# Attention computed by pairs of heads, with gate tiles of the input projection placed among its steps

## The chip, the cores and the metric

The kernel runs on one core of one Trainium2 chip. The metric is the device time of one execution in microseconds (us). Three runs of the kernel before gave 3889.78, 3900.20 and 3900.45 us, median 3900.2 us. The engines are named as in the profile: PE is TensorE, DVE is VectorE, ACT is ScalarE, POOL is GpSimd, SP is SyncE.

## The reference

The reference is a first block (pooling, two convolution branches, a gated feed-forward layer) followed by a second block of two layers. The change lies in the second block. There are 256 latent tokens x and 256 context tokens xc, the model width is 2048. Each layer does, cut to what matters:

```python
u = h @ w_in       # h: normalized x (and xc); columns of u: qa ka va qb kb vb cq ckv kpe z
# a: 8 heads of 64, latent queries see a neighbourhood (bias rpb) plus all context keys
# b: 12 heads of 64 on 4 key heads, window of 128 plus all context keys, one sink logit per head
# c: 6 heads, 192 wide keys (128 + 64 rotary), 128 wide values, from low-rank projections
s = q @ k.T * scale + bias
p = softmax(s)
o = p @ v
y = concat(o_a, o_b, o_c) * silu(z)
x = x + gate * (y @ w_out)
```

Latent queries read 512 keys, context queries read the 256 context keys. In layer 0 both streams are computed (4 blocks of 128 queries), in layer 1 only the latent one (2 blocks), since no later layer reads the context. gate, shift and scale come from c @ w_ada, 24 blocks of 512 columns for both layers.

## The kernel before

All weights come as one stream of quarters of 512 KB (128 x 1024 f32). Each quarter that feeds the projections is split on the fly: ACT copies it to a rounded high part (`hi`, L656), DVE subtracts to get the low part (`lo`, L978), and PE makes three fp32r products for each of 8 chunks (`tile`, L1513 to L1515). A tile of 128 output columns takes two quarters, 48 matmuls, of 512 tokens in layer 0 and of 256 in layer 1 (except keys and values, which always have 512). `hi` and `lo` run AHEAD=3 quarters before PE. Quarters of w_ada are used unsplit by `mod_quarters` (L1540), in four groups of 32 columns; they are woven between tiles by `weave`.

Each layer runs, one after the other: the z tiles (16, `z0`/`z1`; in layer 1 with 32 quarters of w_ada, 8 ahead and 24 among the tiles), the projections of a (12 tiles), attention a, the projections of b (10), attention b, the projections of c (11 tiles and 21 smaller ones), attention c, then the output projection (16 tiles, `out0`/`out1`). A z tile is finished by a sigmoid on ACT (L708) and a product on DVE (L1452).

Attention works by units of one head and 128 queries: a0 has 32 units, b0 48, c0 24, a1 16, b1 24, c1 12. Its steps, in a pipeline several units deep, with two or four PSUM banks for each product:

- PE scores (L1758) into one of four banks; a head of a or b uses 64 of the array's 128 rows, the lower or the upper half
- DVE bias (L1393) or window mask (L1399), maximum (L1401), its negative (L1404; with the sink L1406)
- ACT exponential with row sum (L907; the sink's own, L906)
- DVE reciprocal (L1417) and scaling (L1420)
- PE transposes of the probabilities (L1768), ACT copies them out of PSUM (L916)
- PE values (L1778; 64 of the array's columns for a and b), DVE product with the gate (L1426)

Every engine runs its instructions in program order, and order between engines is set by semaphores: PE's scores of unit n wait for the exponential of unit n-4, its transposes for DVE's scaling, its values for ACT's copy. `projected` and `attention` exist once for each engine and are called in turn:

```python
for name in "abc":
    projected(name, l)
    attention(f"{name}{l}")
```

PE waits between them for the last value transpose (`vt_used`) and for DVE's stage semaphore.

Of the kernel before, what the change touches and what calls it, by code (L numbers as in the profile page):

```python
# [34 lines left out]
S_BANK = (4, 5, 0, 1)  # L35
T_BANK, O_BANK = (6, 2), (7, 3)
BIASES = 4
# [72 lines left out]
Z_MODS = [sum(len(e["pre"]) + len(e["mods"]) for e in w) for w in Z_WEAVE]  # L110
assert FF_GROUPS * FFN_BLOCKS + sum(Z_MODS) // 8 == ADA_BLOCKS

# [12 lines left out]
NQ = _q  # L125

# [7 lines left out]
def _converted():  # L134


    of = []
    for name, nq, _ in PHASES:
        own = set()
        if name == "ffn":  # L140
            own = {FFN_Q * g + pos for g in range(FF_GROUPS) for e in FFN_WEAVE for pos, _ in e["mods"]}
        elif name in ("z0", "z1"):
            l = int(name[1])
            own = {pos for e in Z_WEAVE[l] for pos, _ in e["pre"] + e["mods"]}
        of += [Q0[name] + k for k in range(nq) if k not in own]
    return of
# [64 lines left out]
def build(nc, stream, xT, ctxT, params, consts, natten, out):  # L211
# [68 lines left out]
    probs = sb("probs", [4, 2 * S], F32, "work", 0)  # L280
    probsT = sb("probsT", [3, 4 * P], F32, "work", 8 * KIB)
    bias = sb("bias", [BIASES, S], F32, "q", 16 * KIB)

# [10 lines left out]
    with ExitStack() as ctx:  # L294
# [269 lines left out]
        units, UNITS_OF = [], {}  # L564
        biases = []

        def unit(l, kind, h, qt):
# [3 lines left out]
            u = dict(no=len(units), kind=kind, nk=nk, k0=k0, q0=q0, bias=None, sink=None)  # L571
            if kind == "a":
                a, c = HD * (h % 2), h // 2
                u.update(qk=[(qkv[a:a + HD, c, q0:q0 + P], qkv[a:a + HD, 4 + c, k0:k0 + nk])],
                         v=P * c + a, nv=HD, p0=a, y=c, scale=HD ** -0.5)
                if not ctx_q:
                    u["bias"] = len(biases)
                    biases.append((l, h, qt))
            elif kind == "b":
                c, a = h // 2, HD * (h % 2)  # L580
                t = c // 3
                u.update(qk=[(qkv[a:a + HD, c, q0:q0 + P], qkv[a:a + HD, 6 + t, k0:k0 + nk])],
                         v=P * t + a, nv=HD, p0=a, y=4 + c, scale=HD ** -0.5,
                         sink=H_B * l + B_ORDER[h])
                if not ctx_q:
                    u["swa"] = qt
            else:
                a = HD * (h % 2)
                u.update(qk=[(cqk[:, h, q0:q0 + P], cqk[:, KN + h, k0:k0 + nk]),
                             (cqk[a:a + HD, QROPE + h // 2, q0:q0 + P], cqk[a:a + HD, KR + h // 2, k0:k0 + nk])],  # L590
                         v=P * h, nv=P, p0=0, y=10 + h, scale=QK_C ** -0.5)
            units.append(u)

        for l in range(LAYERS):
            for kind, heads_ in (("a", H_A), ("b", H_B), ("c", H_C)):
                start = len(units)
# [11 lines left out]
        SIG = {"conf": 0, "sconv": 8, "br_c": 16, "br_a": 32, "br_b": 48, "ffn": 64, "z0": 64 + FF_CH, "z1": 80 + FF_CH}  # L608
# [36 lines left out]
        def _(act):  # L645
# [224 lines left out]
            def projected(name, l):  # L870
                tiles_, items = projections(name, l)
                first = T0[f"{name}{l}"]
                for u, todo in enumerate(items):
                    s, nq = tiles_[u][0:2] if u < len(tiles_) else (None, 0)
                    if nq:
                        hi(SQ.index(s) + AHEAD)

                    for it in sorted(todo, key=lambda it: it[0] != "sq"):
                        if it[0] == "fin":
                            root(it[1])  # L880
                        elif it[0] == "vt":
                            n = it[1]
                            act.wait_ge(vt_ready, n + 1)
                            act.activation(vtok[:, :, vts[n][1]:vts[n][1] + P],
                                           psum[:, 7, :].rearrange("p (t c) -> p t c", t=4),
                                           ACT.Copy).then_inc(vt_used, 1)
                        elif it[0] == "cat" and it[2] < len(jobs[it[1]]["cat"]):
                            cat_hi_part(jobs[it[1]], it[2])
                        elif it[0] == "sq":
                            act.wait_ge(psum_free, copied(first, it[4]))  # L890
                            squares(it[1], it[2], it[3])
                    if nq == 2:
                        hi(SQ.index(s) + 1 + AHEAD)

            def attention(name):
                us = UNITS_OF[name]
                for step in range(len(us) + 3):
                    if step < len(us):
                        u = units[us[step]]
# [1178 lines left out]
```

## Time and profile before

| | us |
|---|---|
| median of three runs | 3900.2 |
| the profiled execution | 3891.74 |
| its span | 3889.8 |
| PE busy | 3654.3 (94%) |
| DVE busy | 2197.5 (56%) |
| ACT busy | 1416.3 (36%) |
| mean granted clock of PE | 0.956 |

Busy time of PE is modelled from pipelined matmuls, so it includes short gaps. PEclk 1.00 is 2.4 GHz, 0.50 is 1.2 GHz. "Idle before" is the time in which an engine had nothing to do before an instruction, with what ended it. Stages are named by heads and layer: b0 is attention b of layer 0.

### The profile page before, as it was taken

The page shows a single profiled execution, that of the slowest core. Times are in us where ns is not written, and L with a number is a line of the kernel's source. Part 1 is how long each engine was busy: PE and PEld are TensorE (multiplying, and loading weights), DVE is VectorE, ACT ScalarE, POOL GpSimd, SP SyncE. Part 2 cuts the span into 40 slices and gives each one's busy share as a digit, 9 for nine tenths or more (in the row PEclk, how much of TensorE's full clock was granted, in tenths as well). Part 3 has the DMA queues.
Part 4 walks back from the last instruction along what each step waited for, and adds up shares of the span by engine and source line. Part 5 has one row for each costly group of instructions (what it writes and reads, how often), then busy time and mean ns, then how long its engine had stood idle before and what let it go on. Part 6 is the DMA issues. An engine that isn't in the chain of part 4 may idle for free.

```text
span 3889.8 us, 62805 instructions
## 1 busy us (share of the span) xinstructions
PE 3654.3 (94%) x23040; PEld 3075.4 (79%) x23040; DVE 2197.5 (56%) x3342; ACT 1416.3 (36%) x2126; POOL 583.1 (15%) x558
## 2 busy tenths in 40 slices
PE   7998997999999999999999999998889899999878
PEld 6997996999878788888888676685468687768648
DVE  4566764557646465665426566637643455774744
ACT  4433443445323233344422333423332442443332
POOL 0395995112000000002000000000001000000000
PEclk9998998999999999999999898999899999999979
DMA  4553553555767677767322111021022562212214
GB/s 169 184 182 133 184 182 105 184 194 174 253 213 239 223 245 238 243 230 243 130 98 92 60 65 45 17 76 64 33 88 96 206 232 94 91 39 85 86 43 148
DMA packets 157143, 554.61 MB, mean 143 GB/s; under 512 B 17392, under 2 KB 21488, under 8 KB 156912
## 3 DMA queue, kind: packets, MB, share of 16 engines
q1 hardware_dynamic: 151680, 532.57, 40.7%
q0 software_dynamic: 5232, 18.88, 1.4%
q8 instruction: 155, 2.54, 0.3%
q14 instruction: 76, 0.62, 0.1%
HBM read 545.09 MB, written 6.29 MB: 142 GB/s over the span
## 4 chain that ended last, share of the span: by engine, by line
PE 74%; DVE 8%; POOLq 6%; POOL 5%; ACT 2%; issue 2%; DMA 2%; DVEq 1%; ACTq 0%; SPq 0%
PE psum L1513 19%; PE psum L1514 18%; PE psum L1515 18%; POOLq L1836 6%; PE psum L1758 4%; POOL conv L1837 4%; PE psum L1540 3%; PE psum L1778 3%; DVE rst L1009 2%; PE psum L1768 2%; PE psum L1608 1%; DVE wlo L978 1%; DMA raw<-in_stream 1%; ACT whi L656 1%; PE psum L1550 1%
## 5 line engine op out<-in xcount | busy, mean ns | idle before, releaser
L1513 PE MATMUL psum<-hcat,whi 128*128 128x256 f32 (+1 forms) x5516 | 1743.6, 316 | 66.4 <-DVEq L967 30.9
L1514 PE MATMUL psum<-hcat,whi 128*128 128x256 f32 (+1 forms) x5516 | 1718.8, 312 | 3.2 <-issue 3.2
L1515 PE MATMUL psum<-hcat,wlo 128*128 128x256 f32 (+1 forms) x5516 | 1718.7, 312 | 0.0
L978 DVE TENSOR_TENSOR wlo<-raw,whi 128x1024 fp32r<-128x1024 f32 (+3 forms) x844 | 1034.2, 1230 | 867.2 <-ACT whi L656 840.0
L656 ACT ACTIVATE whi<-raw 128x1024 fp32r<-128x1024 f32 (+3 forms) x844 | 865.5, 1029 | 1280.9 <-PE psum L1515 925.7
L1513 PEld LDWEIGHTS psum<-hcat,whi 128*128 128x128 f32 x5516 | 1067.6, 194 | 197.4 <-issue 107.4
L1514 PEld LDWEIGHTS psum<-hcat,whi 128*128 128x128 f32 x5516 | 1067.7, 194 | 55.8 <-issue 3.8
L1515 PEld LDWEIGHTS psum<-hcat,wlo 128*128 128x128 f32 x5516 | 1066.9, 193 | 56.4 <-issue 3.4
L1835 POOL TENSOR_SCALAR tap<-glu,par 128x255 f32<-128x255 f32 (+9 forms) x180 | 223.0, 1239 | 0.0
L1009 DVE RECIPROCAL rst<-rst 128x512 f32<-128x512 f32 (+1 forms) x65 | 181.1, 2787 | 41.9 <-ACT rst L677 41.9
L1513 PE MATMUL psum<-thirdcat,whi 128*128 128x256 f32 x687 | 201.0, 293 | 0.0
L1514 PE MATMUL psum<-thirdcat,whi 128*128 128x256 f32 x687 | 194.7, 283 | 0.0
L1515 PE MATMUL psum<-thirdcat,wlo 128*128 128x256 f32 x687 | 194.5, 283 | 0.0
L1822 POOL TENSOR_TENSOR thirdcat<-tmp,thirdcat 128x256 fp32r<-128x256 f32 x51 | 54.0, 1059 | 852.5 <-ACT thirdcat L702 852.4
L1837 POOL TENSOR_TENSOR conv<-conv,tap 128x255 f32<-128x255 f32 (+9 forms) x180 | 167.6, 931 | 28.0 <-issue 2.6
L1513 PEld LDWEIGHTS psum<-thirdcat,whi 128*128 128x128 f32 x687 | 131.6, 192 | 50.3 <-issue 41.1
L1778 PE MATMUL psum<-probsT,vtok 128*64 128x128 f32 (+1 forms) x1040 | 159.1, 297 | 11.2 <-ACT probsT L916 10.6
L1906 POOL DMA_DIRECT2D X<-resid_dram x2 | 2.4, 1180 | 1072.7 <-DVEq L967 1072.7
L1540 PE MATMUL psum<-raw,cs 128*32 128x512 f32 x768 | 159.9, 609 | 0.0
L1778 PEld LDWEIGHTS psum<-probsT,vtok 128*64 128x64 f32 (+1 forms) x1040 | 125.1, 160 | 36.2 <-ACT probsT L916 20.6
L907 ACT ACTIVATE probs<-psum,stat 128x512 f32<-128x512 f32 (+1 forms) x156 | 94.8, 607 | 160.0 <-DVE stat L1404 160.0
L1768 PEld LDWEIGHTS psum<-con,probs 128*128 128x128 f32 x520 | 59.3, 151 | 110.2 <-DVE probs L1420 59.9
(179 smaller groups left out, 3250.2 us busy)
## 6 DMA issues: line engine op xcount, KB each, us to landing
raw<-in_stream SPq DMA_DIRECT2D x978, 512.0 KB, 3.9
raw<-in_stream SPq DMA_DIRECT2D x18, 384.0 KB, 3.0
raw<-in_stream SPq DMA_DIRECT2D x24, 256.0 KB, 2.6
X<-in_ctxT POOLq DMA_DIRECT2D x2, 2048.0 KB, 13.4
resid_dram<-X POOLq DMA_DIRECT2D x2, 2048.0 KB, 12.3
bias<-in_natten POOLq DMA_DIRECT2D x32, 128.0 KB, 2.3
X<-resid_dram POOLq DMA_DIRECT2D x2, 2048.0 KB, 9.9
raw<-in_stream SPq DMA_DIRECT2D x16, 192.0 KB, 2.5
```

The source lines that it names most:

```text
L656: act.activation(whi[:, c % HI_SLOTS, 0:n], raw[:, slot, 0:n], ACT.Copy).then_inc(hi_ready, 1)
L978: vec.tensor_tensor(wlo[:, slot, 0:n], raw[:, slot, 0:n], whi[:, c % HI_SLOTS, 0:n].bitcast(F32), ALU.subtract).then_inc(lo_ready, 1)
L1009: vec.reciprocal(r, r)
L1513: pe.matmul(dst, h, cat[:, kk, c0:c0 + width], start=(q == 0 and k == 0), stop=False)
L1514: pe.matmul(dst, h, cat[:, kk, c0 + loff:c0 + loff + width], start=False, stop=False)
L1515: last = pe.matmul(dst, l_, cat[:, kk, c0:c0 + width], start=False, stop=(q == nq - 1 and k == nch - 1))
L1540: last = pe.matmul(psum[32 * g:32 * g + 32, 4 + a // 8 % 2, :], cs[:, j, :], raw[:, s % SLOTS, 512 * k:512 * k + 512], start=(j < 4), stop ...
L1758: last = pe.matmul(psum[:, S_BANK[no % 4], 0:u["nk"]], q, k, start=(m == 0), stop=(m == len(u["qk"]) - 1))
L1778: last = pe.matmul(psum[u["p0"]:u["p0"] + u["nv"], O_BANK[no % 2], 0:P], vtok[:, u["k0"] // P + c, u["v"]:u["v"] + u["nv"]], probsT[:, no ...
L1835: pool.tensor_scalar(tap[:, t % 2, 0:S - t], pick(glu, c, 0, S - t), wt, None, ALU.mult)
L1836: pool.drain()
L1837: pool.tensor_tensor(pick(conv, c, t, S), pick(conv, c, t, S), tap[:, t % 2, 0:S - t], ALU.add)
```

## The change

1. Attention works by pairs of heads. A pair of a or b has one head in each half of the array: its two score products stand next to each other in the program, use rows 0 to 63 and 64 to 127 and write two banks; its value products alternate between columns 0 to 63 and 64 to 127 of one bank. DVE and ACT handle both heads in one instruction where they can (bias, maximum, negative, reciprocal, copy of the transposes, gate product); the exponentials and the scaling stay one for each head.
2. There is one set of banks for pairs (scores 2 and 3, transposes 4 and 5, values 6), for c a second set for scores (0 and 1). The scores of pair p wait for the exponentials of pair p-1 (for c of p-2).
3. Only 2 z tiles (layer 0) or 4 (layer 1) stay ahead of the projections of a. 6 or 5 go beside attention a, 8 or 7 beside attention b. A z tile has four slots of 12 matmuls each, after which PE may do a step of attention: scores of pair p, values of p-2, transposes of p-1. `beside` deals the steps to the slots. ACT and DVE have the same slots in their own programs, with `hi` or `lo` of one quarter at each even slot, the sigmoid of the tile before at slot 0 of a tile, its product at slot 1.
4. The last value transposes and rotations of the projections of a and b are carried into the first slots.
5. The 24 quarters of w_ada among the z tiles of layer 1 go among the tiles of `out0`. All 8 pairs of chunks of the context's normalized input (`hc1`) now fall in the 4 z tiles that are left.

Of the three functions `attend` in the diff the first is ACT's, the second DVE's, the third PE's.

```diff
+Z_SPLIT = [(2, 6, 8), (4, 5, 7)]
-MOD_Z = [0] + [2] * 12 + [0] * 3
-Z_WEAVE = [weave([2] * KD, [0] * KD), weave([2] * KD, MOD_Z, Z_BEFORE)]
+MOD_OUT = [0] + [2] * 12 + [0] * 3
+Z_WEAVE = [weave([2] * Z_SPLIT[0][0], [0] * KD), weave([2] * Z_SPLIT[1][0], [0] * KD, Z_BEFORE)]
+OUT_WEAVE = weave([2] * KD, MOD_OUT)
...
+        def beside(kind, l):
+            n, slots = len(PAIRS_OF[f"{kind}{l}"]), 4 * Z_SPLIT[l]["ab".index(kind) + 1]
+            at = {2 + p * (slots - 3) // (n + 1): p for p in range(n + 2)}
...
+            def attend(p, us):
+                if 1 <= p <= len(us):
+                    transposed(us[p - 1])
+                if p < len(us):
+                    probabilities(us[p])
...
+                for s in range(4 * n):
+                    if s % 2 == 0:
+                        hi(C0[name] + s // 2 + AHEAD)
+                    if s % 4 == 0 and s:
+                        gate(l, z0 + s // 4 - 1)
+                    if s < len(carry):
+                        for_heads(carry[s], T0[f"{kind}{l}"])
+                    if s in at:
+                        attend(at[s], us)
...
+            def attend(p, us):
+                if 1 <= p <= len(us):
+                    norms(us[p - 1])
+                if p >= 3:
+                    gated(us[p - 3])
+                if p < len(us):
+                    maxima(us[p])
...
+                for s in range(4 * n):
+                    if s % 2 == 0:
+                        lo(C0[name] + s // 2 + AHEAD)
+                    if s % 4 == 1 and s > 1:
+                        z_done(l, z0 + s // 4 - 1)
...
+            def scores(no):
+                u = pairs[no]
+                if no:
+                    pe.wait_ge(exp_ready, no if u["kind"] != "c" else max(no - 1, 1))
+                for m, both in enumerate(u["qk"]):
+                    for h, (q, k) in enumerate(both):
+                        last = pe.matmul(psum[:, s_bank(no) + h, 0:u["nk"]], q, k, start=(m == 0),
+                                         stop=(m == len(u["qk"]) - 1))
...
+            def attend(p, us):
+                if p < len(us):
+                    scores(us[p])
+                if p >= 2:
+                    values(us[p - 2])
+                if 1 <= p <= len(us):
+                    transposes(us[p - 1])
```

On ACT, in attention a of layer 1 before, exponentials (L907) and copies (L916) of single units alternate:

```order
L907 ACTIVATE probs,stat<-psum,stat 128x512 x4
L916 ACTIVATE probsT<-psum 128x512
L907 ACTIVATE probs,stat<-psum,stat 128x512
L916 ACTIVATE probsT<-psum 128x512
L907 ACTIVATE probs,stat<-psum,stat 128x512
```

At the same place now (L701 is `hi`, L753 the sigmoid of a z tile, L957 the exponential, L966 the copy):

```order
L957 ACTIVATE probs,stat<-psum,stat 128x512 x2
L701 ACTIVATE whi<-raw 128x1024
L753 ACT_TABLE_LOAD
L753 ACTIVATE tmp<-psum 128x256
L966 ACTIVATE probsT<-psum 128x1024
L957 ACT_TABLE_LOAD
L957 ACTIVATE probs,stat<-psum,stat 128x512 x2
L701 ACTIVATE whi<-raw 128x1024
L966 ACTIVATE probsT<-psum 128x1024
L957 ACTIVATE probs,stat<-psum,stat 128x512 x2
```

The split of a weight quarter and, for each z tile, a sigmoid with two table loads have moved between the exponentials.

On DVE, in the same stage before, one unit follows the other:

```order
L1417 RECIPROCAL stat<-stat 128x1
L1420 TENSOR_SCALAR probs<-probs,stat 128x512
L1426 TENSOR_TENSOR X<-psum,X 64x128
L1393 SCALAR_TENSOR_TENSOR psum<-bias,psum 128x256
L1401 TENSOR_REDUCE stat<-psum 128x1
L1404 TENSOR_SCALAR stat<-stat 128x1
```

And now (L1053 is `lo`, L1524 the product of a z tile, L1497 and L1501 `norms`, L1510 `gated`, L1471 to L1483 `maxima`):

```order
L1480 TENSOR_REDUCE stat<-psum 128x2
L1483 TENSOR_SCALAR stat<-stat 128x2
L1053 TENSOR_TENSOR wlo<-raw,whi 128x1024
L1524 TENSOR_TENSOR X<-psum,tmp 128x256
L1497 RECIPROCAL stat<-stat 128x2
L1501 TENSOR_SCALAR probs<-probs,stat 128x512 x2
L1471 SCALAR_TENSOR_TENSOR psum<-bias,psum 128x2x256
L1480 TENSOR_REDUCE stat<-psum 128x2
L1483 TENSOR_SCALAR stat<-stat 128x2
L1053 TENSOR_TENSOR wlo<-raw,whi 128x1024
L1497 RECIPROCAL stat<-stat 128x2
```

`lo` of a quarter and the product of a z tile stand between the maximum of a pair and its scaling.

On PE, in the same stage, the end of a slot and the start of the next now read (L1638 to L1640 are the z tile, L1889 scores, L1915 values, L1900 transposes); before, nothing of a z tile stood there:

```order
L1638 MATMUL psum<-hcat,whi 128x256
L1639 MATMUL psum<-hcat,whi 128x256
L1640 MATMUL psum<-hcat,wlo 128x256
L1889 MATMUL psum<-qkv 128x512 x2
L1915 MATMUL psum<-probsT,vtok 64x128 x8
L1900 MATMUL psum<-con,probs 128x128 x8
L1638 MATMUL psum<-hcat,whi 128x256
```

The scores of one pair, the values of the one two before and the transposes of the one before it follow 12 or 24 matmuls of a z tile.

## Rows read from the trace of the kernel before

**Rows 1.** Windows: a0, b0, a1, b1, c0, plain tiles of layer 0 and of 1.
```profile
core 0: us, PE busy (x) PEld busy (x) DVE busy (x) ACT busy (x) POOL busy (x), PEclk, DMA share, GB/s
2175.10:2260.70 85.60, 78.62 (x361) 45.45 (x359) 53.41 (x178) 37.39 (x100) 8.60 (x16) 0.86 0.10 31
2380.00:2506.90 126.90, 118.57 (x539) 68.43 (x537) 87.53 (x316) 62.85 (x196) 0.00 (x0) 0.87 0.02 5
3301.70:3355.10 53.40, 45.65 (x233) 27.38 (x231) 33.87 (x98) 23.88 (x52) 8.83 (x16) 0.90 0.16 50
3441.60:3516.00 74.40, 67.06 (x348) 40.43 (x346) 53.76 (x173) 38.37 (x100) 0.00 (x0) 0.93 0.02 8
2756.50:2863.30 106.80, 80.05 (x325) 41.95 (x324) 61.47 (x142) 37.50 (x82) 0.18 (x1) 0.80 0.02 5
...
1900.00:1925.00 25.00, 25.00 (x112) 20.72 (x111) 7.51 (x7) 6.28 (x7) 0.00 (x0) 1.00 0.32 106
3800.00:3825.00 25.00, 25.00 (x211) 25.00 (x210) 12.05 (x14) 9.53 (x9) 0.00 (x0) 1.00 0.51 182
```
**Rows 2.** Timeline in b0: start us, length us, engine, line, what.
```profile
2475.91 0.66 PE L1768 MATMUL psum<-con,probs 128*128 128x128 f32 x4
2476.49 1.09 PE L1778 MATMUL psum<-probsT,vtok 128*64 128x128 f32 x8
2477.41 0.30 ACT L906 ACTIVATE stat<-par,stat 128x1 f32<-128x1 f32 x1 [1.23 <-DVE stat L1406]
2477.51 1.12 PE L1758 MATMUL psum<-qkv 64*128 64x512 f32 x2
2478.27 0.58 ACT L916 ACTIVATE probsT<-psum 128x512 f32<-128x512 f32 x1
```
**Rows 3.** Timeline in the z tiles of layer 1: two quarters of w_ada.
```profile
3100.90 1.06 PE L1540 MATMUL psum<-raw,cs 128*32 128x512 f32 x8
```
**Rows 4.** Groups by line and form, attention: xcount | busy us, mean ns | idle before.
```profile
L1401 DVE TENSOR_REDUCE stat<-psum 128x1 f32<-128x512 f32 x104 | 71.9, 692 | 60.7 <-PE psum L1758 54.5 <-issue 0.4
L907 ACT ACTIVATE probs<-psum,stat 128x512 f32<-128x512 f32 x104 | 70.5, 678 | 134.1 <-DVE stat L1404 134.1
L916 ACT ACTIVATE probsT<-psum 128x512 f32<-128x512 f32 x104 | 60.5, 587 | 6.5 <-PE psum L1768 6.5
L1420 DVE TENSOR_SCALAR probs<-probs,stat 128x512 f32<-128x512 f32 x104 | 50.6, 487 | 8.7 <-issue 0.8
L1401 DVE TENSOR_REDUCE stat<-psum 128x1 f32<-128x256 f32 x52 | 21.8, 420 | 14.7 <-PE psum L1758 14.3
L916 ACT ACTIVATE probsT<-psum 128x256 f32<-128x256 f32 x52 | 19.4, 373 | 5.7 <-PE psum L1768 5.7
L1393 DVE SCALAR_TENSOR_TENSOR psum<-bias,psum 128x256 f32<-128x256 f32 x32 | 13.7, 429 | 30.2 <-PE psum L1758 21.0 <-DMA bias<-in_natten 9.1
```
**Rows 5.** Timeline of ACT at the first z tile of layer 1.
```profile
3071.79 1.04 ACT L656 ACTIVATE whi<-raw 128x1024 fp32r<-128x1024 f32 x1
3072.85 1.28 ACT L708 ACT_TABLE_LOAD   x1
3074.14 0.38 ACT L708 ACTIVATE tmp<-psum 128x256 f32<-128x256 f32 x1
```
**Rows 6.** Timeline of DVE in the z tiles of layer 0.
```profile
1890.65 1.23 DVE L978 TENSOR_TENSOR wlo<-raw,whi 128x1024 fp32r<-128x1024 f32 x1 [1.57 <-ACT whi L656]
```
**Rows 7.** Timeline of PE, first matmul of z1 and of the projections after it.
```profile
3055.86 0.55 PE L1562 MATMUL psum<-hcat,whi 128*128 128x256 f32 x1 [9.32 <-DVE wlo L978]
...
3183.51 0.39 PE L1513 MATMUL psum<-hcat,whi 128*128 128x256 f32 x1 [2.87 <-DVE hcat L1049]
```
**Rows 8.** Windows, columns as in rows 1: two stretches with gaps on PE.
```profile
2675.00:2700.00 25.00, 18.77 (x56) 12.47 (x56) 22.29 (x22) 5.43 (x9) 0.00 (x0) 0.80 0.17 56
...
3025.00:3050.00 25.00, 20.03 (x104) 13.76 (x102) 6.13 (x9) 5.19 (x9) 3.69 (x3) 1.00 0.48 162
```

More of the change, by code:

```diff
@@ L34 @@
 BANKS = 4
[L35 to L37 removed]
+S_BANK, T_BANK, O_BANK = 2, 4, 6
+BIASES = 2
 LATE = 3
@@ L125, with _banks @@
 NQ = _q
+def _banks():
+    banks, free, last = [], [], {}
+    for name, _, nt in PHASES:
+        for t in range(nt):
+            ts = len(banks)
+            b = ts % 2 if name[:2] in ("za", "zb") else ts % BANKS
+            banks.append(b)
+            free.append(BANKS + last[b] + 1 if b in last else 1)
+            last[b] = ts
+    return banks, free
+BANK, FREE = _banks()
 CHUNKS = {}
@@ L561, in copied, with pair_of @@
             return first + t + 1 + BANKS
-        units, UNITS_OF = [], {}
+        pairs, PAIRS_OF = [], {}
         biases = []
-        def unit(l, kind, h, qt):
+        def pair_of(l, kind, c, qt):
             q0 = P * qt
@@ L874, in projected @@
                     s, nq = tiles_[u][0:2] if u < len(tiles_) else (None, 0)
+                    if nq == 0 and name != "c":
+                        break
                     if nq:
                         hi(SQ.index(s) + AHEAD)
[L878 to L891, printed above, removed]
+                    for_heads(todo, first)
@@ new lines, in probabilities @@
+            def probabilities(no):
+                u = pairs[no]
+                b, nk = 2 * (no % 2), u["nk"]
+                act.wait_ge(max_ready, no + 1)
+                if no >= 2:
+                    act.wait_ge(t_ready, no - 1)
+                for h in range(2):
+                    negmax = stat[:, 4 + b + h:5 + b + h]
+                    if u["sink"] is not None:
+                        act.activation(stat[:, 16 + b + h:17 + b + h], pv("sink", u["sink"] + 3 * h), ACT.Exp, bias=negmax)
+                    last = act.activation(probs[:, no % 2, h, 0:nk], psum[:, s_bank(no) + h, 0:nk], ACT.Exp, bias=negmax,
+                                          scale=u["scale"], accum_out=stat[:, 8 + b + h:9 + b + h])
+                last.then_inc(exp_ready, 1)
@@ new lines, in norms @@
+            def norms(no):
+                u = pairs[no]
+                b = 2 * (no % 2)
+                total, rsum = stat[:, 8 + b:10 + b], stat[:, 12 + b:14 + b]
+                vec.wait_ge(exp_ready, no + 1)
+                if u["sink"] is not None:
+                    vec.tensor_tensor(total, total, stat[:, 16 + b:18 + b], ALU.add)
+                    fence()
+                vec.reciprocal(rsum, total)
+                fence()
+                for h in range(2):
+                    pr = probs[:, no % 2, h, 0:u["nk"]]
+                    last = vec.tensor_scalar(pr, pr, rsum[:, h:h + 1], None, ALU.mult)
+                last.then_inc(probs_ready, 1)
```

550 lines of the change are left out of this document (306 added, 244 removed).

## The prediction

> **What bounds the kernel now.** I read the page first (PE busy 94%), then windows cut at the borders of the stages [rows 1]. The reader is to see two kinds of stretch. In plain tiles PE works without a gap at the full clock: 112 matmuls in 25 us in layer 0, 211 in layer 1, so a z tile of 48 takes 10.8 us (48 x 25/112, rounded up, as some records are missing) and 5.7 us. The attention stages take 85.6 (a0), 126.9 (b0), 53.4 (a1) and 74.4 us (b1), with PE busy 85 to 93% of them and a granted clock of 0.86 to 0.93. Then the timeline of b0 [rows 2]: for one unit of 512 keys PE gives 0.58 us to the transposes (2475.91 to 2476.49), 1.02 to the values (to 2477.51) and about 1.05 to the scores, 2.65 in all, while ACT and DVE have slack. So before, attention is bound by PE, plus 10 to 18 us in each stage of filling, emptying and half clock: 16 units of 2.65 and 16 of about 1.85 make 72 of a0's 85.6 us.
>
> **Part 1, the halves of the array.** Two products in different groups of rows or columns may run at once. The trace has this only for four groups of 32 columns [rows 3]: eight records of 512 columns take 1.06 us, where a score of 512 columns alone takes 1.12 for two [rows 2]. I take it over to two groups: the scores of a pair of 512 keys cost 1.1 instead of 2.1 us, the values 1.0 instead of 2.0, the transposes stay at 1.1. A pair costs PE 3.2 instead of 5.3 us, one of 256 keys 1.75 instead of 3.7. The other bound is no overlap, which is a rival below.
>
> **Part 2, the step of a pair as a chain.** This decides. Let N be the end of DVE's scaling of pair p-1. For a pair of a with 512 keys the durations of the new shapes come from one head's rows [rows 4], with what 256 more elements cost (0.27 us in the maximum, 0.21 in the copy):
> - DVE: gate product 0.28, bias on 2x256 0.70 (0.43 + 0.27), maximum over 1024 1.23 (0.69 + 2 x 0.27), negative 0.15, small gaps: ready at N + 2.55.
> - PE transposes 1.1, ACT copy of 1024 1.0: ACT is free at N + 2.35.
> - ACT exponentials, 2 x 0.68: done at E = N + 3.9. Pairs of b have the sink's too, 0.86 a head from 2477.41 to 2478.27 [rows 2], but a smaller mask: E = N + 4.1.
> - reciprocal 0.23 with its gap and scaling 2 x 0.49: 1.2 (b 1.45).
>
> So without anything between, a step takes 5.1 us for a and 5.55 for b. But at each even slot stands the split of a quarter. ACT starts `hi` only behind the exponentials of the pair (1.06 us), DVE's `lo` follows in 1.23 [rows 5, 6], and DVE's scaling, which PE's transposes wait for, is queued behind `lo`: 2.3 us on the chain. Two more things fall on it once in each z tile. The sigmoid of a z tile needs another table than the exponential: in layer 1 it (1.28 + 0.38 [rows 5]) and the product on DVE (0.42, plus a drain) are late by 0.9 us for the scaling; and the table of the exponential, loaded behind the copy, ends at N + 3.6, 1.05 us (a) or 1.3 (b) later than the maximum needs. The z matmuls of a slot (2.7 us in layer 0, 1.43 in layer 1) lie beside this chain, not on it, unless they are longer.
>
> Of the loads the row shows 1.28 us and no more: `hi` ends at 3072.83, the load runs from 3072.85 to 3074.13, the sigmoid starts at 3074.14 [rows 5]. The Trainium skill, ScalarE: Activation LUTs (What ACT_TABLE_LOAD costs), sets about 1.38 us of drain beside the load's 1.28, some 2.66 for a switch, and tells to batch functions by table set, which this change undoes. The trace disagrees on the drain here; a rival below gives it a chance.
>
> Stage by stage, with the slots that `beside` deals:
> - a0 (24 slots, 18 steps, pairs of 512 and 256 keys in turn): 9.5 us until the first scores; 7 intervals of one slot without a quarter at 5.2 (PE's own 2.7 + 1.75 to 3.2 is as long); 6 of one slot with a quarter, 7.4 or 6.5, at 7.0; 4 of two slots at 7.9, where PE is the longer; table loads 3, end 2. Sum 125 us.
> - b0 (32 slots, 26 steps): 9.5 + 11 x 5.4 + 10 x 7.5 + 4 x 8.1 + 5 + 2 = 183 us.
> - a1 (20 slots, 10 steps, nearly all two slots apart, so each with a quarter): a step is 7.4, 8.3 with the product of a z tile, 8.5 with the exponential's table, the last two in turn: 8.4. First pair scaled at 11.3 (its bias comes by DMA only behind the last value transpose), 7 x 8.4, end 4.5: 75 us.
> - b1 (28 slots, 14 steps): 10.5 + 11 x 8.95 + 5 = 114 us.
>
> What they replace: a0 85.6 + 6 z tiles of 10.8 = 150.4; b0 126.9 + 8 x 10.8 = 213.3; a1 53.4 + 5 x 5.7 = 81.9; b1 74.4 + 7 x 5.7 = 114.3 [rows 1]. Gains 25, 30, 7 and 0: 62 us. So about a third of the room is used: PE alone would need 107, 148, 56 and 80 us (z tiles plus pairs plus 2), 169 less than now. In layer 1 PE idles some 2.5 us of each step.
>
> **Part 3, attention c.** No tiles stand beside it. Per pair of 512 keys the overlap of the two rotary products saves 1.0 us on PE, but the chain (transposes, copy, exponentials, scaling, 1.1 + 1.0 + 1.4 + 1.2 and the hand-overs, about 5.1) is close below PE's 5.8, and the pipeline is less deep; at 256 keys the chain is the longer. The half clock at the start stays, since PE's waits at the end of c's projections stay (0.80 over c0 [rows 1]). Between 3 us lost and 12 gained I take 4 gained over c0 and c1.
>
> **Part 4, start of layer 1 and out0.** From z1's first matmul to the projections pass 127.6 us [rows 7]. 12 z tiles leave (68.8 us). The other 4 now hold all 8 chunk pairs of the context, two a tile, each about 1.7 us on ACT beside 2.1 us of `hi` in a tile: about 7 us a tile instead of 5.7 and 6 us of waiting at the end. I get 37 us, so 22 are freed besides the z tiles. The 24 quarters of w_ada cost out0 12 x 1.2 us (1.06 [rows 3] and the changeover) and 3 folds of 0.9: 17 us. Less a dip of the clock behind the wait, net gain 2 us (range -8 to +8). The stream is no limit: out0 would read four quarters in 12 us, 175 GB/s, and plain tiles of layer 1 read 182 GB/s without a gap [rows 1].
>
> **Sum.** 62 + 4 + 2 = 68 us off the profiled execution's 3891.74 (span 3889.8 and 1.9 around): 3824. The three runs lie from 2 below to 9 above it; I add 2: 3826 us, 1.9% under the median.
>
> **Rivals.**
> 1. Full cover: the chain is shorter than I add up, or engines run ahead more than their program order suggests, and PE never waits beside the z tiles. For it: PE has no gap in plain tiles [rows 1]. Against: DVE's queue is strictly in order, and the scaling stands behind `lo` in it. All 169 + 6 us gone gives 3717; half the waits gone 3770.
> 2. The halves don't overlap: two groups of 64 behave unlike four of 32. PE then needs 2.7 + 4.5 = 7.2 us for a step of layer 0 even without a quarter: 18 intervals x 1.9 = 34, and c loses its 4. In layer 1 the chain hides it (2.9 + 5.3 against 8.4). 3864.
> 3. The drain of a table switch is real between exponentials and sigmoids: 1.38 us for each of 22 added loads of the exponential's table, and for the 10 sigmoids of layer 1 that are on the chain, 44 us: 3870. Against it speak [rows 5].
> 4. Slower: the clock. With gaps of 1 to 2.5 us in every step PE is busy only 70 to 75% of the woven stages. One stretch with 75% had 0.80, another with 80% had 1.00 [rows 8]. If the clock falls to 1.2 GHz for good, a slot of layer 0 takes 5.4 and a pair 4.9 on average: 10.3 instead of 6.6 us for 42 intervals, 155 us more, and 3.4 for 18 in layer 1, 61 more: 4042. It eats the whole gain once a third of those stages is at 1.2 GHz.
>
> **Chances.** Forecast 0.60 (own range 3800 to 3850), full cover or half of it 0.14, no overlap 0.12, drain 0.05, clock 0.07, others 0.02. Range 3768 to 3872: it leaves out full cover, the upper part of rival 3 and rival 4. A difference within 0.3% (12 us) can't be told from none. Faster by more: the forecast, rivals 1 and 2 and half of 3, 0.87; same 0.06; slower 0.07.
>
> **What would show it.** Right: 22 more loads of the exponential's table and 26 of the sigmoid's, 1.28 us each with no gap behind; DVE's scaling starting right behind `lo` in even slots, PE idle 1 to 2.5 us before the transposes (L1900) and released by the scaling (L1501), steps of 7 us in a0, 8.4 in a1 and 9 in b1; score records of a pair starting together; clock near 1.00 in all four stages. Wrong: if PE's idle before L1900 sums to less than 30 us the cover was better; if the second score starts only as the first ends, rival 2; a clock under 0.9 in the woven stages, rival 4; stages a1 and b1 longer than before together with their z tiles, and the whole above 3872, would mean the chain is longer than I made it.

## The result, and the profile after

Over 20 runs of each, the kernel with the change takes 3901.4 us in the median (3895.7 to 3908.3), the kernel before 3889.7 (3877.7 to 3901.0): ratio 1.0027, 95% interval 1.0017 to 1.0037. It is slower by some 10 us, where I had forecast 3826, 1.9% faster. The profiled execution has a span of 3901.0 us. One more execution of the kernel before, timed beside e5 to e8, took 6071.5 us at a mean granted clock of 0.618 and is left out of the ratios as slow. The first view is the windows of the stages, cut as the stages of the sum (z tiles beside them included), then attention c0 and c1 from first scores to last values. Columns are those of [rows 1].

```profile
core 0: us, PE busy (x) PEld busy (x) DVE busy (x) ACT busy (x) POOL busy (x), PEclk, DMA share, GB/s
2023.50:2154.20 130.70, 112.45 (x644) 82.39 (x643) 57.26 (x120) 62.72 (x112) 4.33 (x8) 0.95 0.19 65
2275.00:2473.10 198.10, 161.16 (x916) 117.68 (x915) 84.54 (x205) 96.82 (x209) 0.00 (x0) 0.93 0.12 43
3216.50:3305.30 88.80, 64.33 (x466) 54.24 (x464) 39.97 (x70) 42.58 (x66) 4.33 (x8) 0.87 0.27 85
3393.20:3533.80 140.60, 99.29 (x672) 83.13 (x670) 58.11 (x119) 65.94 (x119) 0.00 (x0) 0.83 0.16 53
2747.60:2831.30 83.70, 64.97 (x312) 44.55 (x312) 27.43 (x71) 23.34 (x60) 0.00 (x0) 0.83 0.00 1
3741.20:3789.10 47.90, 37.73 (x192) 23.97 (x192) 15.95 (x35) 14.28 (x30) 0.00 (x0) 0.93 0.00 1
```

a0, b0, a1 and b1 sum to 558.2 us. Before, with the z tiles that have moved into them, they took 559.9 [rows 1]. So 1.7 us came of the 62 that were forecast there. Attention c0 took 72.3 us before by the same cut (2779.25 to 2851.55) and takes 83.7; c1 took 53.4 and takes 47.9.

The waits of PE from a0 to b1 (engine, its line, releaser: us in total, times, longest) name the new wait at once; rows of other waits are left out:

```profile
engine line waited for: us in total, times, longest us
PE psum L1915 <- DVE X L1510: 107.6, 55, 4.3
PE psum L1889 <- ACT probs L957: 23.5, 19, 4.4
...
PE psum L1900 <- DVE probs L1501: 7.7, 6, 2.5
```

My chain ended at the transposes (L1900), which wait for the scaling (L1501). PE does not wait there. It waits one instruction earlier, ahead of the value products (L1915), and for the gate product (L1510). A step of b1 shows why; these are rows of the timelines of ACT, DVE and PE in order of time, the z tile's matmuls left out.

```profile
3445.38 0.88 DVE L1501 TENSOR_SCALAR probs<-probs,stat 128x512 f32<-128x512 f32 x2 [0.43 <-issue]
...
3446.60 1.45 PE L1915 MATMUL psum<-probsT,vtok 128*64 128x128 f32 x16 [2.99 <-DVE X L1510]
...
3451.95 0.68 ACT L957 ACTIVATE probs<-psum,stat 128x512 f32<-128x512 f32 x1
...
3452.61 1.06 ACT L701 ACTIVATE whi<-raw 128x1024 fp32r<-128x1024 f32 x1
3453.09 1.13 PE L1889 MATMUL psum<-qkv 64*128 64x512 f32 x4
3453.68 1.28 ACT L753 ACT_TABLE_LOAD   x1
3453.70 1.23 DVE L1053 TENSOR_TENSOR wlo<-raw,whi 128x1024 fp32r<-128x1024 f32 x1 [5.37 <-ACT whi L701]
3455.39 0.42 DVE L1524 TENSOR_TENSOR X<-psum,tmp 128x256 f32<-128x256 f32 x1 [0.47 <-ACT tmp L753]
...
3456.43 0.88 DVE L1501 TENSOR_SCALAR probs<-probs,stat 128x512 f32<-128x512 f32 x2
3457.23 0.28 DVE L1510 TENSOR_TENSOR X<-psum,X 128x128 f32<-128x128 f32 x1
3457.66 1.97 PE L1915 MATMUL psum<-probsT,vtok 128*64 128x128 f32 x16 [3.45 <-DVE X L1510]
3459.57 1.70 PE L1900 MATMUL psum<-con,probs 128*128 128x128 f32 x8
3461.30 1.02 ACT L966 ACTIVATE probsT<-psum 128x1024 f32<-128x1024 f32 x1 [5.94 <-PE psum L1900]
```

PE's step is scores of p, values of p-2, transposes of p-1. There is one bank for outputs, so the values of p-2 wait for the gate product of p-3 (L1909). DVE's step is `norms(p-1)`, `gated(p-3)`, `maxima(p)`. The gate product's input had been ready for 9.2 us (since 3448.05, where the values before end), but the product stands behind the scaling, and the scaling stands behind the exponentials, `hi`, `lo` and, in this step, the product of a z tile. So the values start only after the scaling (3457.66), and the transposes, which could have started at 3457.3, follow at 3459.57, 2.3 us late. They carry this on to the copy, to the next exponentials and so around the loop. From values to values the step is 11.06 us long (3446.60 to 3457.66), where I had 8.95. It is a usual one: the steps of b1 are 11.1 us long on average, those of a1 9.8, of a0 7.4 and of b0 7.7.

### The profile page after: what moved, and what is told of

It reads as the page before. It is cut to its first block, busy times and chain, and to the rows that moved or that the text cites. A ratio compares the mean times of both kernels' runs of the same rounds, so it can differ in the third digit from the quotient of the medians.

```text
span 3901.0 us, 61624 instructions
## 1 busy us (share of the span) xinstructions
PE 3540.0 (91%) x23040; PEld 3036.2 (78%) x23040; DVE 2123.6 (54%) x2954; ACT 1462.2 (37%) x2092; POOL 574.8 (15%) x542
## 4 chain that ended last, share of the span: by engine, by line
PE 60%; DVE 10%; issue 8%; ACT 7%; POOLq 6%; POOL 5%; DVEq 2%; DMA 1%; ACTq 0%; SPq 0%
PE psum L1638 16%; PE psum L1639 16%; PE psum L1640 16%; POOLq L2004 6%; POOL conv L2005 4%; PE psum L1668 3%; PE psum L1915 3%; PE psum L1900 2%; DVE rst L1084 2%; DVE wlo L1053 2%; ACT probs L957 2%; ACT whi L701 2%; PE psum L1736 1%; DVEq L1039 1%; DVE probs L1501 1%
## 5 line engine op out<-in xcount | busy, mean ns | idle before, releaser
L1638 PE MATMUL psum<-hcat,whi 128*128 128x256 f32 (+1 forms) x5516 | 1757.4, 319 | 74.3 <-DVEq L1042 30.7
L1640 PE MATMUL psum<-hcat,wlo 128*128 128x256 f32 (+1 forms) x5516 | 1720.0, 312 | 0.0
L1053 DVE TENSOR_TENSOR wlo<-raw,whi 128x1024 fp32r<-128x1024 f32 (+3 forms) x844 | 1031.2, 1227 | 1017.3 <-ACT whi L701 981.1
L701 ACT ACTIVATE whi<-raw 128x1024 fp32r<-128x1024 f32 (+3 forms) x844 | 866.5, 1030 | 1239.6 <-PE psum L1640 854.7
L1638 PEld LDWEIGHTS psum<-hcat,whi 128*128 128x128 f32 x5516 | 1072.3, 194 | 207.4 <-issue 97.5
L1640 PEld LDWEIGHTS psum<-hcat,wlo 128*128 128x128 f32 x5516 | 1070.0, 194 | 55.6
L1915 PEld LDWEIGHTS psum<-probsT,vtok 128*64 128x64 f32 (+1 forms) x1040 | 86.5, 173 | 163.2 <-issue 160.8
L1915 PE MATMUL psum<-probsT,vtok 128*64 128x128 f32 (+1 forms) x1040 | 106.2, 318 | 117.4 <-DVE X L1510 115.4
L1638 PE MATMUL psum<-thirdcat,whi 128*128 128x256 f32 x687 | 200.7, 292 | 0.0
L1640 PE MATMUL psum<-thirdcat,wlo 128*128 128x256 f32 x687 | 194.1, 283 | 0.0
L966 ACT ACTIVATE probsT<-psum 128x1024 f32<-128x1024 f32 x78 | 68.9, 884 | 330.2 <-PE psum L1900 330.2
L1638 PEld LDWEIGHTS psum<-thirdcat,whi 128*128 128x128 f32 x687 | 131.4, 191 | 50.3 <-issue 39.4
L1736 PE MATMUL psum<-sq,con 128*128 128x512 f32 (+1 forms) x248 | 109.5, 557 | 33.2 <-ACT sq L717 25.5
```

The costliest lines, as they stand in the source:

```text
L701: act.activation(whi[:, c % HI_SLOTS, 0:n], raw[:, slot, 0:n], ACT.Copy).then_inc(hi_ready, 1)
L1053: vec.tensor_tensor(wlo[:, slot, 0:n], raw[:, slot, 0:n], whi[:, c % HI_SLOTS, 0:n].bitcast(F32), ALU.subtract).then_inc(lo_ready, 1)
L1638: pe.matmul(dst, h, cat[:, kk, c0:c0 + width], start=(q == 0 and k == 0), stop=False)
L1640: last = pe.matmul(dst, l_, cat[:, kk, c0:c0 + width], start=False, stop=(q == nq - 1 and k == nch - 1))
L1736: pe.matmul(dst, sel[p0:p1], src, start=(m == 0), stop=(m == len(J["srcs"]) - 1)).then_inc(sq_used, 1)
L1915: last = pe.matmul(dst, v, probsT[:, h, P * c:P * c + P], start=(c == 0), stop=(c == n - 1))
```

## The experiments

From here G is the theory just told (named for the gate product), K the rival that the lower clock of the four stages is the cause, L that only what I had on the chain is on it. Ratios are to the kernel before, run on the same chip. The table has the time from the first scores to the last values of each stage in the profiled execution.

| kernel | median us | ratio, 95% | a0 | b0 | c0 | a1 | b1 | c1 |
|---|---|---|---|---|---|---|---|---|
| before, no z tiles inside | 3889.7 | 1 | 82.7 | 123.6 | 72.3 | 50.5 | 71.0 | 53.4 |
| the change | 3901.4 | 1.0027 (1.0017 to 1.0037) | 122.7 | 190.1 | 83.7 | 84.6 | 136.5 | 47.9 |
| e1 gate product first | 3822.7 | 0.9825 (0.9802 to 0.9849) | 111.3 | 169.5 | 65.7 | 77.2 | 123.0 | 40.2 |
| e2 lo later | 3831.5 | 0.9839 (0.9812 to 0.9865) | 108.5 | 161.5 | 83.6 | 76.9 | 119.9 | 48.1 |
| e3 both | 3770.6 | 0.9688 (0.9666 to 0.9711) | 104.4 | 149.2 | 65.7 | 69.4 | 106.0 | 40.3 |
| e5 e3, z product later | 3735.6 | 0.9600 (0.9578 to 0.9622) | 102.5 | 149.8 | 65.7 | 59.0 | 85.3 | 40.5 |
| e6 e5, table ahead | 3723.3 | 0.9568 (0.9547 to 0.9590) | 101.7 | 145.6 | 64.6 | 55.7 | 81.4 | 40.4 |
| e7 no table switches | 3861.6 | 0.9930 (0.9907 to 0.9954) | 116.2 | 179.7 | 82.9 | 78.9 | 121.3 | 48.0 |
| e9 the change, filled | 3895.9 | 0.9997 (0.9982 to 1.0011) | 125.9 | 190.0 | 82.8 | 87.2 | 131.8 | 48.1 |
| e10 values in turn | 3920.6 | 1.0067 (1.0045 to 1.0090) | 123.6 | 189.8 | 82.8 | 93.3 | 145.7 | 50.1 |
| e4 pairs alone | 4007.2 | 1.0291 (1.0263 to 1.0319) | 109.4 | 169.6 | 80.4 | 66.0 | 104.9 | 50.0 |
| e8 alone, filled | 3938.0 | 1.0119 (1.0094 to 1.0144) | 91.4 | 144.4 | 80.4 | 56.7 | 86.4 | 48.0 |
| e11 alone, filled, gate first | 3872.5 | 0.9945 (0.9919 to 0.9971) | 80.5 | 127.7 | 64.5 | 51.6 | 76.6 | 41.5 |

**e1, the wait itself.** DVE's step only:

```diff
-                if 1 <= p <= len(us):
-                    norms(us[p - 1])
                 if p >= 3:
                     gated(us[p - 3])
+                if 1 <= p <= len(us):
+                    norms(us[p - 1])
```

> In DVE's step the gate product of pair p-3 (gated, L1510) now stands ahead of the scaling of pair p-1 (norms). Nothing else is changed. Theory G: PE's value products of pair p-2 wait for the single output bank, which that gate product frees; behind the scaling it puts values (1.1 us), product (0.28) and hand-overs, 1.6 us, on the chain of each step. Then the value products lie beside `lo` and scaling: some 50 steps with a quarter save 1.6, some 20 without 0.6, the 22 of attention c about 1.2: 115 us off the kernel with the change, near 3786, and PE's idle before L1915 put down to L1510 (115 us there) falls under 20. Theory K (the stages are long because TensorE's granted clock is lower in them, 0.83 to 0.93): the order of two DVE instructions changes nothing, under 15 us off. Theory L (only the split of the quarters stands on the chain, as predicted): also under 15 us off, since the wait moves to the transposes.

Swapping two neighbours in DVE's order takes 2.0% off the kernel with the change (79 us by the ratios), two thirds of what I expected; K and L allowed 15 us. Each of the six stages is shorter, c0 by 18 us, so c0's loss was this wait too. The 79 us hold what the clock gives back when PE waits less: it rose in every stage (a0 0.95 to 0.99, b0 0.93 to 0.98, a1 0.87 to 0.92, b1 0.83 to 0.87, c0 0.83 to 0.93, c1 0.93 to 0.96). The part that is missing is in the waits, over the whole span:

```profile
PE psum L1915 <- DVE X L1510: 51.3, 35, 3.6
```

51.3 us, not under 20: the product now stands ahead of the scaling, but still behind `lo` and the z tile's product of its slot. PE in b1 of e1 still waits for it:

```profile
3381.17 1.97 PE L1915 MATMUL psum<-probsT,vtok 128*64 128x128 f32 x16 [1.37 <-DVE X L1510]
...
3391.12 1.98 PE L1915 MATMUL psum<-probsT,vtok 128*64 128x128 f32 x16 [2.49 <-DVE X L1510]
```

**e2 and e3, `lo` off the chain.** In DVE's `z_beside`:

```diff
-                    if s % 2 == 0:
-                        lo(C0[name] + s // 2 + AHEAD)
+                    if s % 2 == 0 and s:
+                        lo(C0[name] + s // 2 - 1 + AHEAD)
...
+                lo(C0[name] + 2 * n - 1 + AHEAD)
                 z_done(l, z0 + n - 1)
```

> Beside attention a and b DVE makes each low part (lo) two slots later, 2 quarters ahead of PE instead of 3, so that ACT's hi of that quarter is long done; DVE can make it while ACT computes the exponentials (1.4 us). The gate product stays behind the scaling. Theories G and L agree here: hi 1.06 and lo 1.23 leave the chain of about 48 steps, 110 us off at most, 80 to 110 off the kernel with the change: near 3805. Theory K: nothing but a few us. If lo is then short for PE (its matmuls wait for wlo), little is gained.

> Both edits: gate product ahead of the scaling, lo two slots later. Theory G: the step is exponentials 1.4, scores 1.13, values 1.1, transposes 1.1, copy 1.0, about 5.9, and the z matmuls of a slot lie beside it; PE's own work of a step (6.0 to 6.2) is as long, so PE is nearly full in the woven stages; the exponential's table still costs up to 1.28 for each of 26 z tiles. Near 3745, 3725 to 3780, and the stages a0, b0, a1, b1 together 430 instead of 558 us. Theory L: as e2 alone. Theory K: as the kernel with the change.

e2 takes 1.9% off (73 us), less than the 80 to 110 expected, and c0, which has no `lo`, keeps its 83.6. e3 takes 3.4% off (132 us) and misses its 3745 by 26, just inside its range; the four stages, cut as the 558 above, came to 454 us and not to 430. So both waits are on the chain, and little of them overlaps (79 + 73 against 132). What e3 still waited for is on DVE, from a0 to b1:

```profile
DVE X L1524 <- ACT tmp L753: 55.3, 17, 4.4
```

The product of a z tile (L1524) stood ahead of the attention step and waited up to 4.4 us for a sigmoid, which ACT makes behind the exponentials, `hi` and a table load; in the kernel with the change this row was only 12.2 us, because `lo` ahead of it was late already.

**e5 and e6, the z tile's gate.** e5 moves `z_done` behind `attend` in DVE's slot. e6 adds one instruction on ACT:

```diff
                     if s % 4 == 0 and s:
                         gate(l, z0 + s // 4 - 1)
+                        act.activation(stat[:, 20:21], par[:, 0:1], ACT.Exp, scale=0.0)
```

> On top of e3: DVE makes the product of a z tile (L1524) behind the step of attention in its slot instead of ahead. In e3 DVE idled 44 us in a0, a1 and b1 before that product for the sigmoid, which ACT makes only behind the exponentials, hi and a table load of 1.28 us, and the gate product that frees the output bank stood behind it. If that wait is on the chain, some 30 us go in layer 1 and a few in layer 0: near 3738. If it is beside the chain, 3770 as e3.

> On top of e5: right behind each sigmoid beside attention ACT computes an exponential of one column that nobody reads, so that the exponential's table (1.28 us) is loaded while ACT waits for the transposes anyway, and not between the copy and the next exponentials. 22 loads leave the chain if the chain runs through ACT there: 20 to 28 us off e5, near 3715. If PE's own work is the bound by then, less than 10.

e5 came out as expected (3735.6 for 3738; a1 10 us and b1 21 us shorter than in e3). e6 gained 12 us more, about half of what I expected: a1 and b1 fell by 3.3 and 3.9, b0 by 4.2, a0 by 0.8. Its windows for a0, b0, a1 and b1 show PE nearly full at last:

```profile
2034.80:2136.50 101.70, 99.05 (x606) 72.09 (x605) 56.91 (x119) 59.91 (x114) 3.23 (x6) 0.98 0.22 73
2265.20:2410.80 145.60, 139.78 (x878) 100.53 (x877) 83.50 (x201) 93.81 (x214) 0.00 (x0) 1.00 0.16 52
3133.80:3189.50 55.70, 51.20 (x430) 41.55 (x429) 37.82 (x68) 40.64 (x67) 3.91 (x8) 0.97 0.37 120
3281.50:3362.90 81.40, 75.45 (x638) 61.75 (x637) 54.35 (x114) 64.31 (x123) 0.00 (x0) 0.98 0.25 83
```

PE is busy 92 to 97% of them. With the slots ahead of the first scores (8.1 us in layer 0, 4.3 in layer 1) they are 409 us, near the 391 that the prediction had for PE alone. e6 beats both kernels, by 4.3% the one before.

**e7, what the table switches cost.** e7 leaves out the sigmoid of the z tiles beside attention.

```diff
-                of_tile(ACT.Sigmoid, tmp, BANK[T0[name] + t],
+                of_tile(ACT.Sigmoid if name[1] not in "ab" else ACT.Copy, tmp, BANK[T0[name] + t],
```

> The kernel with the change, but the z tiles beside attention are copied instead of put through the sigmoid, so that no table changes there: 26 loads of the sigmoid's table and 22 of the exponential's go. This leaves out the sigmoid of those tiles. By my prediction's price, 1.05 to 1.3 for each of 22 loads of the exponential's table on the chain and 0.9 for the sigmoids of layer 1: some 35 us off, 3866. By the rival of a drain (2.66 for a switch, the Trainium skill, ScalarE: Activation LUTs): some 75 us off or more, 3825.

It took 1.0% off, 38 us, where I had priced 35. By the groups of ACT (those of the kernel with the change are below) e7 has 24 loads less for the sigmoid (6 instead of 30) and 20 less for the exponential (6 instead of 26), where I had expected 26 and 22; 44 x 1.28 is 56 us, so two thirds of that came off the kernel:

```profile
L753 ACT ACT_TABLE_LOAD x30 | 38.5, 1283 | 10.2 <-PE psum L1640 5.7 <-PE psum L1692 4.1
L956 ACT ACT_TABLE_LOAD x14 | 18.0, 1283 | 0.2
...
L957 ACT ACT_TABLE_LOAD x12 | 15.4, 1283 | 0.2
```

**e4 and e8, pairs without z tiles, and the clock.** e4 sets `Z_SPLIT` to (16, 0, 0) for both layers and runs `attend` of a and b in a plain loop, as for c. e8 adds to `transposes`:

```diff
+                if u["kind"] != "c":
+                    for _ in range(3):
+                        pe.matmul(psum[:, 7, 0:u["nk"] // 2], cv("ident"), con[:, CO["sin"]:CO["sin"] + u["nk"] // 2],
+                                  start=True, stop=True)
```

> Pairs of heads in the two halves stay, but all 16 z tiles of a layer stand ahead of the projections of a again, and nothing is between the steps of attention a and b. The 24 quarters of w_ada stay with the output projection. Theory G: a step of 512 keys is scaling 1.2, gate product 0.3, values 1.2, transposes 1.1, copy 1.0, exponentials 1.4 and hand-overs 0.3, 6.5 us (b 6.9), of 256 keys about 3.9, longer than two heads took before (5.3 and 3.7): a0 about 90 (before 85.6), b0 140 (126.9), a1 57 (53.4), b1 88 (74.4). So pairs alone are slower than the kernel before by some 40 us, about 3935, and slower than the kernel with the change. My prediction's account (chain 5.1 to 5.55, values not on it) gives 8 x 5.1 + 8 x 3.5 + 8, 77 us for a0, 115 for b0, 47 for a1 and 72 for b1: some 30 us faster than before, 3865. Theory K predicts a faster kernel too, since PE has 100 us less to do in these stages.

> The pairs alone of e4, with three matmuls more on PE behind the transposes of each pair of a and b (128 rows, half as many columns as the pair has keys, into a bank that nobody reads), while PE waits 2.8 us for the exponentials. It adds some 1.6 us of work to a step of 512 keys. Theory K in its part: e4's steps are 8.5 us instead of my 6.5 since the granted clock is 0.60 to 0.71 in these stages, and scores, values and transposes take 2.08, 1.97 and 1.97 instead of 1.13, 1.09 and 1.09 (2.7 us a step, all of it on the chain). If PE's idle time is what brings the clock down, the filled kernel runs these stages over 0.85 and is 60 to 90 us faster than e4, about 3930, though PE has 80 us more to do. If the clock stays, it is slower than e4, 4010 to 4060.

e4 was far slower than G's 3935: 4007. The chain is the one of G, but its parts on PE take nearly twice as long: in b1 the values 1.97 or 1.98 us and the transposes 1.97 in every step, the scores 2.08 in every second one (1.14 in the others). The steps are 8.7 and 8.4 us in turn. b1 of e4, first its window, then the scores and values of one of the longer steps:

```profile
3538.40:3643.30 104.90, 65.05 (x337) 42.04 (x337) 38.22 (x95) 35.00 (x86) 0.00 (x0) 0.61 0.00 1
```
```profile
3583.43 2.08 PE L1892 MATMUL psum<-qkv 64*128 64x512 f32 x4 [2.81 <-ACT probs L957]
3585.43 1.97 PE L1918 MATMUL psum<-probsT,vtok 128*64 128x128 f32 x16
```

And b1 of e8, with the three matmuls that nobody reads (L1908; L1922 are the values, L1903 the transposes):

```profile
3486.80:3573.20 86.40, 59.60 (x409) 40.62 (x409) 37.70 (x95) 35.02 (x86) 0.00 (x0) 0.92 0.00 1
```
```profile
3524.48 1.13 PE L1892 MATMUL psum<-qkv 64*128 64x512 f32 x4 [1.52 <-ACT probs L957]
3526.16 1.09 PE L1922 MATMUL psum<-probsT,vtok 128*64 128x128 f32 x16 [0.56 <-DVE X L1510]
3527.19 1.09 PE L1903 MATMUL psum<-con,probs 128*128 128x128 f32 x8
3528.12 1.46 PE L1908 MATMUL psum<-con 128*128 128x256 f32 x6
3531.10 1.13 PE L1892 MATMUL psum<-qkv 64*128 64x512 f32 x4 [1.52 <-ACT probs L957]
```

The granted clock rises from 0.61 to 0.92, the step falls from 8.4 and 8.7 us to 6.6 (G: 6.9), and the kernel is 69 us faster although PE has more to do. G's stages (90, 140, 57, 88) are within 5 us of those of e8 (91.4, 144.4, 56.7, 86.4).

**e9, the clock in the change itself.** The same three matmuls in the kernel with the change.

> The kernel with the change, and behind the transposes of each pair of a and b three matmuls on PE into a bank that nobody reads (as in e8, 1.6 us for 512 keys at full clock). It sizes what the lower granted clock (0.83 to 0.94 there) costs the change itself. In b1 about a third of the time is at 1.2 GHz, where scores, values and transposes take 3 us more a step; over the four stages about 40 us. The filling stands where PE waits 2 us and more in layer 1, but in layer 0, where PE is 81 to 85% busy, part of it adds to the path. Clock a second cause beside theory G: 10 to 35 us off the kernel with the change, near 3880, and b1 under 128 instead of 136.5. Clock the main cause: 60 us off or more. Clock without effect: slower by 10 to 60 us.

0.3% faster by the ratios (12 us, and 5.5 by the medians; the two intervals just part), the lower edge of what I expected of a second cause. In b1 the clock rises only from 0.83 to 0.87, and b1 is 131.8 us, not under 128; a0 and a1 got 3 us longer. The six stages together did not move (665.8 for 665.6), so where the 12 us come from is not shown. (Of the 6.2 us between the two profiled spans, 4.5 lie between the end of c0 and the start of a1, where no filling stands.) In layer 0 the clock rose to 0.99 and 0.97, but PE was 86 and 81% busy there before the filling, and a0 got longer. K as the main cause falls by e1, where 79 us went and K allowed 15. What the lower clock costs the change in layer 1 is not measured: the filling left it at 0.87 to 0.88.

**e10, the order of the two halves.** `values` issues one head after the other.

> The kernel with the change, but the value products of a pair of a or b are issued for one head and then for the other, instead of alternating between the two halves of the columns. If the alternation is what makes the halves overlap, 16 products take 2.0 instead of 1.09 us (8 of 256 keys 1.1 instead of 0.6); 26 pairs... in all 20 of 256 keys and 40 of 512 in a and b, so 0.9 x 40 + 0.5 x 20 = 46 us more. By theory G the values are on the chain in nearly every step, so nearly all of it shows: slower than the kernel with the change by 35 to 46 us, 3940. If values lie beside the chain, as my prediction had it, under 10 us. If the order doesn't matter for the overlap, nothing.

0.4% slower, 16 us, well under what was expected. Three sizes were off. Sixteen products in turn take 1.55 us at full clock and not 2.0 (first row, e10; second, the kernel with the change), so alternating is worth 0.46. At the lower clock it is worth 0.88: 2.85 us (third row, b1 of e10) against 1.97 in the step of b1 above. And eight products of 256 keys take 0.67 us in turn and 0.66 alternating at full clock, so they lose nothing.

```profile
2437.20 1.55 PE L1914 MATMUL psum<-probsT,vtok 128*64 128x128 f32 x16 [0.29 <-DVE X L1510]
```
```profile
2071.41 1.09 PE L1915 MATMUL psum<-probsT,vtok 128*64 128x128 f32 x16
```
```profile
3441.35 2.85 PE L1914 MATMUL psum<-probsT,vtok 128*64 128x128 f32 x16 [3.54 <-DVE X L1510]
```

The stages tell where it counts. In a1 and b1 the values of the 20 pairs sum to 49.8 us instead of 30.4, 19 us more, and the two stages are 17.9 us longer: there the values are on the chain nearly always. In a0 and b0 they sum to 7.8 us more, but the two stages grew by only 0.6. The clock was 0.03 higher there than in the kernel with the change (0.97 for 0.94 and 0.96 for 0.93 from first scores to last values), which may hide a part; so for layer 0 e10 does not show the values on the chain. The wait of the values for the gate product is on it there too: e1 took 11 us off a0 and 21 off b0.

**e11, pairs alone in the right order.** e8 with the edit of e1.

> e8 (pairs alone, filled) with the gate product ahead of the scaling. It tells what pairs are worth without the z tiles beside them, once the order is right and the clock is up. Step: exponentials 1.4 (b 1.75), scores 1.13, values 1.1, transposes 1.1, copy 1.0, 0.2 between: 5.9 (b 6.3) for 512 keys, about 3.4 for 256. a0 81 instead of 89, b0 127 instead of 143, a1 52 instead of 54, b1 80 instead of 83, c0 and c1 together 25 shorter: some 50 us off e8, 3890, the same as the kernel before. Then all that e6 gains over before comes from the z tiles that lie beside the steps. If pairs alone beat before by over 30 us, that is wrong.

0.6% faster than before (21 us), 18 us more than expected and under the 30 that would have spoken against it. Against before, c0 and c1 together gain 19.7 us, a and b together lose 8.6. So pairs of a and b, run like this and with the filling in, are worth nothing by themselves. e6 is 149 us faster than e11. It differs by the z tiles beside the steps, by the edits of e2, e5 and e6, which only order them, and by the filling that it does without; no run separates these.

## Why the prediction was wrong

**The step that failed** is in Part 2: the chain went from DVE's scaling of p-1 to "PE transposes 1.1" as if nothing stood between. I priced values and gate product ("values 1.0", "gate product 0.28") as work of PE and DVE, not as links: values(p-2) stand ahead of transposes(p-1) on PE, wait for gated(p-3), and that stands behind norms(p-1) on DVE. The time from the scaling's end to the exponentials' end, E - N, which I had as 4.1 in b, is 6.3 in the step above (from 3446.26 to 3452.61, where `hi` starts). Of the 2.2 us more, about 1.0 is the wait: the gate product and values of full length (1.09) ahead of the transposes, less the gaps that I had allowed. The other 1.2 are the lower clock, 0.9 in the transposes (1.97) and the rest in the values (1.45). The wait is in the kernel (`pe.wait_ge(o_used, no)`, L1909); DVE's order was in the diff and PE's in the rows of the order, both shown ahead of the prediction. The Trainium skill, PSUM — Partial Sum Buffer (Engine vs sequencer instructions), says that the queues of ScalarE, VectorE and GpSimdE are strict FIFO; e1 agrees, with 79 us for two neighbours on VectorE.

**How much of the miss it is.** With the gate product put ahead of the scaling, which takes the most of this wait off my chain, e1 measures 3822.7 us, and 3826 was forecast. By stage this is partly luck: with the slots ahead of the scores e1 takes 119.3, 177.6, 81.5 and 127.3 us for my 125, 183, 75 and 114, 9 more in all, and c gains 20 where I had 4. Layer 1 was too short in my account since `lo` and the z tile's product still hold the gate product there (e3, e5) and the clock is 0.87 to 0.92.

The second term that was off is the clock, which I had near 1.00 in all four stages; it was 0.95, 0.93, 0.87 and 0.83. Since there are two levels, a mean of 0.83 means 1.2 GHz for 34% of the time. By the windows, an estimate, a0 to b1 with their z tiles ran at 1.2 GHz for 78 us before (the z tiles at a clock of 1.00 [rows 1]), 112 us in the kernel with the change and 56 us in e1; all six attention stages ran so for 147 us with the change and 68 in e1. PE's instructions take up to twice as long there (values 1.97 for 1.09), so of the 79 us that e1 took off at most 40 came by way of the clock. No run separates this part of the miss from the wait.

**Point by point.**
- Part 1, the halves overlap: right. The scores of a pair take 1.13 us, the values 1.09 at full clock. Rival 2 falls.
- `hi` and `lo` on the chain at even slots: right (e2, 73 us).
- Table loads: right in price (e7, 38 us) and within 2 in each count. Rival 3, a drain of 1.38 us per switch, falls: by it e7 would have gained some 75 us. The Trainium skill, ScalarE: Activation LUTs (What ACT_TABLE_LOAD costs) sets that drain; here the row shows 0.01 us between `hi`'s end (3453.67 in the step above) and the load.
- Part 3, c: I had 4 us gained over both; c0 lost 11.4 and c1 gained 5.5, so 5.9 were lost, by the same wait; with e1's order c0 and c1 gain 6.6 and 13.2.
- Part 4: 253.5 us from the first matmul of out0 in layer 0 to the projections of a1, before 320.1 less 68.8 for the z tiles, so 2 us lost where I had 2 gained. The start took 42.1 us for my 37, out0 18.9 more for my 17.
- Rival 4, the clock: its sign, under 0.9, came in layer 1 (0.87 in a1, 0.83 in b1), but filling PE's idle time bought back only 12 us net (e9), not the 216 of the rival. In e4, without z tiles, it was worth 69 us.
- Rival 1, full cover: it didn't happen, but it was there to be had: e6 is 3723, my figure for it 3717.
- What would show it: I had set PE's idle time ahead of the transposes (L1900) under 30 us as the sign of better cover. It was 7.7 us from a0 to b1, and the cover was worse: the wait had moved one instruction ahead, to the values. The prediction also named a1 and b1 longer than before with their z tiles, and the whole above 3872, as the sign that the chain is longer than I made it. Both came (88.8 for 81.9, 140.6 for 114.3, 3901).
- The chance: I gave 0.07 to slower, all of it to the clock. Every other term had a range; the list of links in the chain had none.

The span grew by 11.2 us: -1.7 in a and b, +5.9 in c, +2.2 in Part 4; some 5 us lie between the stages. The stretch from a0 to b0 is 1.5 us longer, from b0 to c0 2.2, from the projections of layer 1 to a1 1.9 and from a1 to b1 1.4, and the others together are some 2 shorter; why is not shown.

## What to carry to other kernels

When the chain of a software pipeline is drawn, write down for each engine the full order of its step and every wait in it, and follow each wait to what stands ahead of its signal on the other engine; an instruction whose own input is long ready is still a link if it stands behind one that is late. Releases of a single buffer belong at the front of a step, bulk work that others don't wait for behind the step, and a function table is best loaded where its engine waits anyway. Before forecasting a gain from cover, swap neighbours on paper: if an order exists that shortens the chain, the given one may not have it.

## What the runs showed of the hardware

- PE can be made faster by giving it more work: with 2.81 us of idle time ahead of the scores in each step of 8.4 to 8.7 us the granted clock of b1 was 0.61, values and transposes took 1.97 us each and the scores 2.08 in every second step; with 1.5 us of matmuls put into that idle time it was 0.92, and they took 1.13, 1.09 and 1.09 (e4, e8).
- The values of two heads in two column halves take less than twice the time of one head even when issued one after the other: 1.55 us for 16 matmuls, against 1.09 alternating (e10) and 1.02 for the 8 of one head before [rows 2]. At the lower clock it is 2.85 against 1.97. With 256 keys the order makes no difference (0.67 and 0.66).
- Hiding a load of a function table by a one-column activation works: e6 has four loads more than e5 (60 for 56 of the sigmoid's and the exponential's) and is 12 us faster, since 22 of them now stand behind the sigmoids.
